# The value products of a step, and the sample's, moved behind the scores of the next step on TensorE

## The reference

```
s1, a1, g1, s2, a2, g2 = silu(c) @ w_ada + b_ada        # modulation, 6 x 1024
h  = RMSNorm(x) * (1 + a1) + s1
q, k, v, hc, B, C, ga, gb = h @ w_in
z[t, s] = q[t] . k[s] / 8 + bias[head]                  # 8 heads of 64
A[t, s] = sigmoid(z[t, s]) * prod_{s < j < t} (1 - sigmoid(z[t, j]))    # s < t
o  = A @ v                                              # stick-breaking attention
y  = B * causal_conv3(C * hc)
x += g1 * ((sigmoid(ga) * (o @ w_att) + sigmoid(gb) * (y @ w_conv)) @ w_o)
x += g2 * (relu(h2 @ w1) ** 2 @ w2)
```

## Time and profile before

| | us |
|---|---|
| median of 3 runs (lowest, highest) | 1799.37 (1795.88, 1800.89) |
| the profiled execution, its own time | 1793.89 |
| its span, first to last instruction | 1792.1 |
| TensorE busy | 1697.5 (95%) |
| VectorE busy | 879.7 (49%) |
| GpSimd busy | 675.6 (38%) |
| ScalarE busy | 307.7 (17%) |
| mean granted TensorE clock, share of full speed | 0.979 |

### The profile page before, as it was taken

One profiled execution on the slowest core, in us unless ns is written; L12 is line 12 of the kernel. 1 busy time (PEld: TensorE's weight loads), 2 busy tenths in 40 slices (PEclk: granted clock), 3 DMA queues, 4 the chain that ended last, 5 costly groups with the idle time before them and its releaser, 6 DMA issues.

```text
span 1792.1 us, 30076 instructions
## 1 busy us (share of the span) xinstructions
PE 1697.5 (95%) x12030; PEld 1565.8 (87%) x12030; DVE 879.7 (49%) x1453; ACT 307.7 (17%) x597; POOL 675.6 (38%) x390
## 2 busy tenths in 40 slices
PE   6679999999989999999999989999999999999999
PEld 4679877777867777779998889999999999999998
DVE  2333346556454545444772286545454545454543
ACT  3123321111111111113111152101010102020200
POOL 2025325435434445443332354333333333333331
PEclk9689999999999999999999999999999999999999
DMA  6211235655655666625422101111111111111112
GB/s 243 95 59 48 83 145 178 212 170 174 229 189 186 234 215 202 235 93 208 145 104 88 36 24 60 43 41 47 48 48 48 48 48 48 48 48 47 39 45 97
DMA packets 72506, 196.85 MB, mean 110 GB/s; under 512 B 8081, under 2 KB 8210, under 8 KB 72370
## 3 DMA queue, kind: packets, MB, share of 16 engines
q1 hardware_dynamic: 67682, 179.77, 29.8%
q10 hardware_dynamic: 4688, 15.18, 2.3%
HBM read 175.41 MB, written 19.50 MB: 109 GB/s over the span
## 4 chain that ended last, share of the span: by engine, by line
PE 89%; DVE 5%; issue 2%; ACT 2%; POOL 1%; DMA 1%; ACTq 0%; SPq 0%; DVEq 0%; POOLq 0%
PE bank L626 73%; PE bank L737 2%; PE bank L761 2%; PE bank L804 2%; PE bank L780 2%; PE bank L750 1%; PE bank L663 1%; PE bank L675 1%; PE bank L855 1%; DVE AT L1273 1%; PE bank L702 1%; PE bank L650 1%; PE bank L676 1%; PE bank L677 1%; POOL wl L543 1%
## 5 line engine op out<-in xcount | busy, mean ns | idle before, releaser
L541 POOL TENSOR_TENSOR wh<-raw,zero 128x1024 fp32r<-128x1024 f32 x116 | 220.8, 1903 | 740.3 <-PE bank L626 643.8
L543 POOL TENSOR_TENSOR wl<-raw,wh 128x1024 fp32r<-128x1024 f32 x116 | 286.2, 2467 | 9.1
L626 PE MATMUL bank<-hH,wh 128*128 128x352 f32 x816 | 276.7, 339 | 2.0 <-POOL wl L543 2.0
L626 PE MATMUL bank<-hL,wh 128*128 128x352 f32 x816 | 262.9, 322 | 0.0
L626 PE MATMUL bank<-hH,wl 128*128 128x352 f32 x816 | 262.6, 322 | 0.0
L626 PE MATMUL bank<-h2H,wh 128*128 128x352 f32 x768 | 249.3, 325 | 5.7 <-DVE h2L L1443 4.7
L626 PE MATMUL bank<-hidH,wh 128*128 128x352 f32 x768 | 247.7, 323 | 0.0
L626 PE MATMUL bank<-h2H,wl 128*128 128x352 f32 x768 | 247.2, 322 | 0.0
L626 PE MATMUL bank<-h2L,wh 128*128 128x352 f32 x768 | 247.1, 322 | 0.0
L1413 DVE SCALAR_TENSOR_TENSOR act<-bank,mods,act 128x352 f32<-128x352 f32 (+1 forms) x216 | 122.3, 571 | 253.1 <-PE bank L626 252.7
L626 PE MATMUL bank<-hidH,wl 128*128 128x352 f32 x768 | 246.3, 321 | 0.0
(11 more groups left out here) (155 smaller groups left out, 2537.5 us busy)
## 6 DMA issues: line engine op xcount, KB each, us to landing
raw<-in_weights SPq DMA_DIRECT2D x168, 512.0 KB, 3.6
ring<-in_cache_k SPq DMA_DIRECT2D x128, 256.0 KB, 3.8
ring<-in_cache_v SPq DMA_DIRECT2D x128, 256.0 KB, 3.5
gate_scratch<-gt ACTq DMA_DIRECT2D x16, 528.0 KB, 3.0
act<-gate_scratch SPq DMA_DIRECT2D x16, 528.0 KB, 4.6
xt<-in_xT SPq DMA_DIRECT2D x8, 528.0 KB, 8.5
act<-in_xT SPq DMA_DIRECT2D x8, 528.0 KB, 4.5
out_yT<-act SPq DMA_DIRECT2D x8, 528.0 KB, 2.7
```

The lines of the kernel that those rows point to most:

```text
L541: mark(pool.tensor_tensor(wh[u % 2][:, :], src[:, :], zero[:, 0:1].to_broadcast([P, 1024]), ALU.add))
L543: pool.tensor_tensor(wl[u % 2][:, :], src[:, :], wh[u % 2][:, :].bitcast(F32), ALU.subtract)\
L626: mm = pe.matmul(out, x, y, start=n == 0, stop=n == end)
```

## The change

On TensorE the value products of the last step and of the last sample item no longer end the tick that turned them: they are issued in the next tick, behind that tick's scores and ahead of its first dense group. `out_block`, `sample_out` and `sample_gathered` move on VectorE to the next tick too, behind its `keep_and_scan`. `SLOTS` follows, and so does the place at which a page of cached values counts as used. One wait is added on VectorE: the running product of the step before must have read its buffer before 1 - beta is written into it.

```
-SLOTS = ("scores", "dense_a", "sturn", "sscore", "turn", "dense_b", "ada", "av", "sav")
+SLOTS = ("scores", "av", "sav", "dense_a", "sturn", "sscore", "turn", "dense_b", "ada")

-            out.append(("v", TURN_AT[k], place(k, "sav")))
+            out.append(("v", TURN_AT[k], place(k + 1, "sav")))

             for k in range(TICKS):                       # TensorE
                 if k < NSTEP:
                     scores(k)
+                if 1 < k <= NSTEP + 1:
+                    values(k - 2)
+                if k - 1 in TURN_AT:
+                    sample_values(TURN_AT[k - 1])
+                    if ITEMS[TURN_AT[k - 1]][1] == PAGES - 1:
+                        gather(ITEMS[TURN_AT[k - 1]][0])
                 if k in DENSE_A:
                     dense(DENSE_A[k], hH, hL)
...
                     ada(ADA_AT[k], ada_ps)
-                if 0 < k <= NSTEP:
-                    values(k - 1)
-                if k in TURN_AT:
-                    sample_values(TURN_AT[k])
-                    if ITEMS[TURN_AT[k]][1] == PAGES - 1:
-                        gather(ITEMS[TURN_AT[k]][0])

                     dve.wait_ge(S["beta_done"], x + 1)   # VectorE, keep_and_scan
+                    if k >= 2 and STEPS[k - 1].c:
+                        dve.wait_ge(S["scan_done"], x - 1)

                 if k < NSTEP:                            # VectorE, the loop over the ticks
                     keep_and_scan(k)
+                if 1 < k <= NSTEP + 1 and STEPS[k - 2].final:
+                    out_block(k - 2)
+                if k - 1 in TURN_AT and TURN_AT[k - 1] in (PAGES, NITEM - 1):
+                    sample_out(TURN_AT[k - 1] // (PAGES + 1))
+                    sample_gathered(TURN_AT[k - 1] // (PAGES + 1))
...
                     ada_copy(ADA_AT[k], ada_ps)
-                if 0 < k <= NSTEP and STEPS[k - 1].final:
-                    out_block(k - 1)
-                if k in TURN_AT and TURN_AT[k] in (PAGES, NITEM - 1):
-                    sample_out(TURN_AT[k] // (PAGES + 1))
-                    sample_gathered(TURN_AT[k] // (PAGES + 1))
```

## The result

The changed kernel is slower by 8.5 us: 1806.95 us (1803.06 to 1809.97, 8 runs) against 1798.40 (1795.51 to 1801.45, 8 runs) of the kernel before beside it, ratio 1.0047 with a 95% interval of 1.0033 to 1.0061. The profiled execution took 1806.42 us (span 1804.6) where that of before took 1793.89. All of it lies in the ticks: the first dense group of tick 47 starts at 812.46 us for 800.04, 12.4 later, and behind it nothing moved by more than 0.5 us.

What follows compares the result with a forecast made beforehand. TensorE, busy 95% of the span, was taken to bound the kernel through its order and waits. 8.8 + 1.7 + 3.4 - 4.3 + 0.6 = 10.2 us slower, on the median 1799.4, gave 1809.6 us; range 1801 to 1816.

Steps and rivals of the forecast that it cites:

- the clock, which had no term: TensorE's granted clock: half speed noted behind the stalls of ticks 10 and 21, but no cost in the sum.
- 18 ticks x 0.49 = 8.8: Ticks with modulation product and second dense group: scores wait for the exposed copy, 0.49 us lost each, 8.8 together.
- 11 ticks, 1.7: Ticks with modulation product but no second dense group: the stall stays, scores wait for the copy, 1.7 us lost together.
- Ticks 14 and 20, 3.4: Convolution ahead of the copy: values no longer fill that wait, 2.02 us lost in tick 14, 1.37 in 20.
- 6 ticks, -4.3: Ticks with neither modulation product nor second dense group: the next scores run in the stall, 4.3 us gained.
- the gather, +0.6: Tick 46: sample_out behind a running product makes the gather idle 0.6 us more, bounds 0 and 1.3.
- Rival 1: All 17 ticks with a values stall: scores fill it, the copy being no obstacle; 12.1 us faster, 1787.3; 5%.
- Rival 2: Ticks 10, 21, 34: running product no longer meets GpSimd's split; up to 9.3 us back, 1800.3; 14%.
- the 0.05 of the prediction: Running product against GpSimd's split: a 0.05 us shift would remove a stall whole or make a new one.
- Rival 3: About 9 ticks: earlier 1 - beta and running product meet GpSimd's split, delaying copy or turn; 19 us slower, 1818; 10%.
- the first kind of tick: The 18 ticks with modulation product and second dense group, where nothing now covers the copy; 8.8 us lost.

Runs made afterwards that it cites:

- run 7: The change with VectorE's copy of the modulation product made twice in each tick from m = 16 on; 1812.88 us, ratio 1.0083 to the kernel before.
- run 1: The change with the modulation product in the next dense group's bank, so the second head's scores wait for no copy; 1787.01 us, ratio 0.9938 to the kernel before.
- run 12: The change with the gathers behind their tick's first dense group and sample_gathered behind the copies of the turned weights; 1802.43 us, ratio 1.0022 to the kernel before.
- run 3: The change with unread dense products put into its five longest TensorE stalls; 1797.66 us, ratio 1.0005 to the kernel before.
- run 4: The kernel before with 14 and 18 unread dense products ahead of the values of ticks 10 and 21; 1793.96 us, ratio 0.9981 to the kernel before.
- run 9: The kernel before with only values and out_block moved, plus the modulation product in the next dense group's bank; 1773.77 us, ratio 0.9865.
- run 5: The kernel before with only values and out_block moved, the sample's values and gather left at the tick's end; 1780.48 us, ratio 0.9904.

## Why the prediction was right, and where its sum was not

The sign and the mechanism hold, and the total does by the medians: 10.2 us were forecast, 8.5 measured. The total is partly luck. All terms of the sum are order, and the order cost 5.9; the clock, which had no term, brought the rest.

- **18 ticks x 0.49 = 8.8:** measured 9.3. Sixteen lie between 0.38 and 0.54; ticks 25 and 40 have 0.75 and 0.69, because the sample's running product ran beside the second half of GpSimd's split there and not the first (in tick 25 2.65 us from 557.59, 0.04 behind the start of L543; 2.02 before, beside L541) and so made the copy later. Doubling the copy (run 7) and taking it out of the way (run 1) both confirm the cause.
- **11 ticks, 1.7:** measured -1.0, a step that failed. I had the copy end behind the stall as it was before. But with the values behind them, the scores of a step start some 2 us earlier before its first dense group, and all that hangs on them is earlier: in tick 26 GpSimd's product (L568) ended before the sample's 1 - beta began (POOL idle for 2.85 us before 571.61, for 0.69 at this place before), which took 0.23 us instead of 0.60, and the turned weights were copied 1.44 us behind the modulation product's start instead of 1.88. Ticks 13, 26 and 37 gain 0.25 to 0.54 by that; ticks 5, 7, 23, 29 and 31 lose 0.11 to 0.17, about what was forecast; ticks 2 and 10 gain 0.18 and 0.32, and tick 34 is as it was.
- **Ticks 14 and 20, 3.4:** measured 1.9 of order. The new wait is as long as read, the copy ends 3.07 us after TensorE is free for 3.05. Against that, tick 14 became shorter in its middle: the turn had waited 0.78 us for VectorE's copy of the sample's turn (L1284), which the eviction of the first dense group held up (its small copy L1331 took 1.07 us beside GpSimd's product, and takes 0.18 now); now it doesn't, and 2.19 us instead of 3.00 lie between the sample's turn and the second dense group. Tick 14 has 1.7 us of clock besides.
- **6 ticks, -4.3, and the gather, +0.6:** measured -4.5 in sum over these ticks, for -3.7: 1.06 in ticks 15 and 39 as forecast; 0.82 in 18 and 42, where 0.43 was forecast, since there too the sample's 1 - beta now comes clear of GpSimd's product and takes 0.23 us instead of 0.56; 0.89 in tick 21 for 0.64; and tick 45, with the gather's longer wait in it, +0.1. The gather idled 0.9 more (1.71 for 0.81), where I took 0.6: the running product ended 4.2 us after the scores began (794.09 to 798.30) for the 3.1 that I read, because of the 1.77 us of 1 - beta in the rows of run 12.
- **The clock, which had no term:** 6.8 us in the profiled execution, 3.6 in the mean. This is the step that was wrong by kind. I named the lower clock behind the stalls of ticks 10 and 21, and then took the stalls' lengths as all that could change. The change left the long waits nearly as long: TensorE idles 3.02, 3.16 and 3.15 us behind ticks 10, 21 and 34, for 3.24, 4.14 and 3.37 before. It turned the 1.16 of tick 15 into one of 2.26, as the copy of tick 14 told, and the gather's 0.81 into 1.71. All five had the half clock behind them, for two before. Runs 3 and 4 show that these stalls bring it: in those that are filled, it is gone.
- **Rival 1** (scores fill the stalls, 12.1 faster) had 5%, as the copy stands in the way. With the copy out of the way it came true: run 1 is 14.2 us of order below before.
- **Rival 2** (meetings dissolve): not in ticks 10, 21 and 34; at 663.36 in tick 34 the running product takes 2.59 us as in the earlier trace rows. The Trainium skill's rule ("SBUF — State Buffer", Who interferes with whom) agrees with the rows on ticks 25 and 26, where one meeting became longer and one was undone. But the shifts that did it were 1.4 and 2.5 us (the start of the sample's 1 - beta against GpSimd's instruction), not the 0.05 of the prediction.
- **Rival 3** (new meetings, 19 slower): they did come. Seven of the sample's running products that took 2.02 us take 2.62 to 2.65, and the 96 parts of 1 - beta take 54.0 us for 42.9. Nearly all is covered by the dense groups, as I had argued against it; what isn't is the 1 - beta of tick 46, for which the second gather waited.

```profile
663.36 2.59 DVE L1260 TENSOR_TENSOR_SCAN skb<-skb,skb,zero 128x129 f32<-128x129 f32 x1
...
557.59 2.65 DVE L1260 TENSOR_TENSOR_SCAN skb<-skb,skb,zero 128x129 f32<-128x129 f32 x1
```

What I didn't see at all is that the change is two changes. Moving the values is worth 15 us of order; moving the sample's values as well gives it all back and more, 20.9 us. With the copy out of the way the same move costs 7.9 (run 1 has 1743.3, run 9 1735.4). So 13.0 us are the cover of the copy, which the sample's values had been; my own term for the first kind of tick says as much, "now nothing does", without drawing the conclusion. The other 7.9 remain without that wait, and 3.7 of them lie in the 6 ticks that have no copy. They fit what the sample's values do there: they wait for nothing late, so at the end of the tick they fill part of the stall, and behind the values they can't. It stays open why the same stall brings the half clock in one execution and not in another. The 3.37 us of tick 34 had none behind them in the profile of before, and the same 3.37 had in run 4; the 3.15 of tick 22 had it in the change and had none in runs 7 and 12. The spread of before's mean clocks, 0.974 to 0.980, is of that size. Nor does its cost simply follow the stalls' length, as the mean of run 7 shows.

## What to carry to other kernels

Before moving work into a stall, list what it covered where it stood: here 2 us of products hid a 0.43 us copy, and half of them would have been enough. And move only what waits: the sample's values, which waited for nothing, did more where they were. A buffer that is shared by two users far apart in the order becomes a wait when the order brings them together; doubling the suspected operation shows in one run, tick by tick, where it lies on the path. And price a TensorE stall with the clock behind it: unread products that can start at once are a cheap test of how much is clock and how much is wait. In the change, all five stalls that were filled had both parts; they were 1.71 to 3.16 us long.

## What the runs showed of the hardware

- The granted clock fell to 0.50 (1.2 GHz) behind single waits in a stream that is otherwise some 99% busy (in the change 7.4 us idle over the ticks besides the five stalls): behind 3.02 us in tick 11 and 1.71 at the second gather, while in before a dozen waits of 1.1 to 1.8 us and one of 3.37 had none behind them. 14 unread products (2.45 us) in the wait of tick 11 kept it at full speed.
- The spread of this kernel's runs is the clock: over before's 69 executions the time has a standard deviation of 2.9 us and the order one of 0.9, and filling five stalls narrowed the change's range from 6.9 us (8 runs) to 2.3 (12 runs).
- The scores of the two heads run at the same time, 0.92 us for both when undisturbed (697.69 in run 5). Parted by a wait of 0.26, as in the rows of ticks 26 and 27, each takes 0.9 by itself, and from the first head's start to the values it is 1.98 us for 0.85.
